# Branch sum before weight piece: a new order of the splits in the last two branch steps of a two-layer decoder

## The reference

```python
h = rms_norm(x, norm1_g[l])
P = h @ w_in[l]                        # all queries, keys, values and gates
o_a, o_b, o_c = window_attention, block_attention, gated_linear_attention   # each 256 x 512
g = sigmoid(gates)                     # 3 gates of 256 x 1024
y = g[0] * (o_a @ w_branch_a) + g[1] * (o_b @ w_branch_b) + g[2] * (o_c @ w_branch_c)
x = x + y @ w_o
x = x + FFN(rms_norm(x, norm2_g[l]))   # layer 0: SwiGLU of 2816; layer 1: top 2 of 8 experts of 1408
```

## Time and profile before

| what | value |
|---|---|
| median of 3 runs | 1080.41 us (1075.01 to 1085.00) |
| profiled execution: time | 1086.16 us |
| profiled execution: span of the trace | 1084.40 us |
| busy TensorE, VectorE, ScalarE (share of the span) | 98%, 48%, 37% |
| mean granted TensorE clock | 0.978 of full speed |

### The profile page before, as it was taken

How to read it: one execution, slowest core, us unless ns; L and a number is a source line. 1 busy time by engine, 2 the same in 40 slices (tenths; PEclk the granted TensorE clock), 3 DMA queues, 4 the chain that set the end, 5 groups by cost and what they waited for, 6 DMA issues and landing times.

```text
span 1084.4 us, 21913 instructions
## 1 busy us (share of the span) xinstructions
PE 1057.7 (98%) x9653; PEld 873.4 (81%) x9653; DVE 519.7 (48%) x751; ACT 402.6 (37%) x619; POOL 17.0 (2%) x61
## 2 busy tenths in 40 slices
PE   8999999998999999999999999799999999999996
PEld 7998999998999999999899999796554563563552
DVE  5565776576467565456578655735112111111112
ACT  5554655535354453457346553331111011011012
POOL 3000000000000000000000000010000000000000
PEclk8999999999999999999999999888999999999999
DMA  6553643664556475555345449696999999999991
GB/s 212 173 163 91 185 147 117 182 207 141 170 176 179 152 221 197 164 159 172 111 141 162 145 133 343 209 350 218 390 401 398 404 402 398 402 404 398 399 363 40
DMA packets 131278, 255.38 MB, mean 236 GB/s; under 512 B 7505, under 2 KB 80241, under 8 KB 131186
## 3 DMA queue, kind: packets, MB, share of 16 engines
q1 hardware_dynamic: 130322, 252.41, 66.8%
q10 hardware_dynamic: 864, 1.59, 0.4%
HBM read 252.93 MB, written 1.05 MB: 234 GB/s over the span
## 4 chain that ended last, share of the span: by engine, by line
PE 89%; DMA 4%; DVE 2%; SPq 2%; ACT 2%; issue 1%; ACTq 0%; DVEq 0%
PE ps L1579 33%; PE ps L1574 16%; PE ps L1576 15%; PE ps L1575 15%; PE ps L1568 3%; PE ps L1570 3%; PE ps L1569 3%; SPq L553 2%; DMA e_ring<-in_moe_w_down 2%; ACT w_hi L690 1%; DMA raw<-in_w_o 1%; DVE w_lo L984 1%; PE ps L1787 1%; DMA x<-in_x 1%; DVE xhat L1241 0%
## 5 line engine op out<-in xcount | busy, mean ns | idle before, releaser
L984 DVE TENSOR_TENSOR w_lo<-raw,w_hi 128x1536 fp32r<-128x1536 f32 (+2 forms) x157 | 248.6, 1604 | 141.0 <-ACT w_hi L690 140.8
L690 ACT ACTIVATE w_hi<-raw 128x1536 fp32r<-128x1536 f32 (+2 forms) x157 | 210.5, 1361 | 158.3 <-DMA raw<-in_w_in 81.4
L1574 PE MATMUL ps<-hT_hi,w_hi 128*128 128x256 f32 (+1 forms) x752 | 217.4, 289 | 8.0 <-DVE hT_lo L1033 3.6
L1575 PE MATMUL ps<-hT_lo,w_hi 128*128 128x256 f32 (+1 forms) x752 | 213.6, 284 | 0.0
L1576 PE MATMUL ps<-hT_hi,w_lo 128*128 128x256 f32 (+1 forms) x752 | 213.6, 284 | 0.0
L1579 PE MATMUL ps<-e_ring,xe 128*32 128x352 f32 (+2 forms) x2560 | 199.6, 462 | 0.0
L1579 PEld LDWEIGHTS ps<-e_ring,xe 128*32 128x32 f32 x2560 | 106.0, 110 | 83.3 <-issue 56.0
L1574 PEld LDWEIGHTS ps<-hT_hi,w_hi 128*128 128x128 f32 (+1 forms) x752 | 143.1, 190 | 12.5 <-issue 6.9
L1576 PEld LDWEIGHTS ps<-hT_hi,w_lo 128*128 128x128 f32 (+1 forms) x752 | 143.2, 190 | 0.5
L1575 PEld LDWEIGHTS ps<-hT_lo,w_hi 128*128 128x128 f32 (+1 forms) x752 | 143.2, 190 | 0.4
L1579 PE MATMUL ps<-e_ring,ehT 128*32 128x512 f32 x880 | 101.3, 593 | 1.1 <-DMA e_ring<-in_moe_w_down 1.1
(11 more groups left out here) (330 smaller groups left out, 1426.7 us busy)
## 6 DMA issues: line engine op xcount, KB each, us to landing
e_ring<-in_moe_w_gate SPq DMA_DIRECT2D x64, 704.0 KB, 12.5
e_ring<-in_moe_w_up SPq DMA_DIRECT2D x64, 704.0 KB, 12.8
e_ring<-in_moe_w_down SPq DMA_DIRECT2D x88, 512.0 KB, 12.3
raw<-in_w_in SPq DMA_DIRECT2D x56, 768.0 KB, 4.3
raw<-in_w_in SPq DMA_DIRECT2D x20, 512.0 KB, 3.6
raw<-in_ffn_w_gate SPq DMA_DIRECT2D x12, 768.0 KB, 4.5
raw<-in_ffn_w_up SPq DMA_DIRECT2D x12, 768.0 KB, 4.4
raw<-in_ffn_w_down SPq DMA_DIRECT2D x12, 768.0 KB, 4.4
```

The costliest lines, as they stand in the source:

```text
L690: act.activation(slot(n, "hi", k), slot(n, "raw", k), ACT.Copy).then_inc(hi_done, 1)
L984: dve.tensor_tensor(slot(n, "lo", k), slot(n, "raw", k), slot(n, "hi", k).bitcast(F32), ALU.subtract).then_inc(lo_done, 1)
L1574: pe.matmul(out, wh, hi, start=first, stop=False, skip_group_check=True)
L1575: pe.matmul(out, wh, lo, start=False, stop=False, skip_group_check=True)
```

## The change

Branch steps 7 and 8 are entered in `BEHIND` with 0 splits at their head, so that their one split comes after their own work. On ScalarE the copy of a group of `y` moves from the end of its own step into the next one (group 0 into step 7, group 1 into step 8, group 2 to the head of step 0 of the output projection).

```diff
-BEHIND = {("wof", 2): 1, ("down", DOWN_END[0]): 0, ("down", DOWN_END[1]): 0}
+BEHIND = {("branch", 7): 0, ("branch", 8): 0, ("wof", 2): 1, ("down", DOWN_END[0]): 0, ("down", DOWN_END[1]): 0}
...
+            def y_high(l, s):
+
+                k0, k1 = OCOLS[s][0] // P, sum(OCOLS[s]) // P
+                act.wait_ge(y_ready, y_banks(l, s))
+                act.activation(hT_hi[:, k0:k1, :], xT[:, k0:k1, :], ACT.Copy).then_inc(y_hi_done, 1)
+
...
                     n, p, a, _ = FIRST[l, step]
+                    if name in ("wo", "wof") and i == 0:
+                        y_high(l, 2)
                     for u in splits_before(l, step):
                         split_hi(u)
...
-                    elif name == "branch" and i >= 6:
-                        k0, k1 = OCOLS[i - 6][0] // P, sum(OCOLS[i - 6]) // P
-                        act.wait_ge(y_ready, y_banks(l, i - 6))
-                        act.activation(hT_hi[:, k0:k1, :], xT[:, k0:k1, :], ACT.Copy).then_inc(y_hi_done, 1)
+                    elif name == "branch" and i >= 7:
+                        y_high(l, i - 7)
```

## The result

The changed kernel takes 1066.89 us (median of 4 runs, 1064.39 to 1068.31) against 1078.60 us for the kernel before (median of 4, 1075.01 to 1085.0): ratio 0.9875, 95% interval 0.9844 to 0.9905, so 13.5 us less (10.2 to 16.8). The two medians by themselves lie 11.7 us apart; the ratio on record is used from here on. Both kernels ran again on another chip: ratio 0.9864 (0.9848 to 0.988), 14.7 us less (13.0 to 16.4). So the changed kernel is faster, by a little over 1%. The forecast was 1066.2 us, 14.2 us less. The profiled execution after is 1068.31 us, its span 1066.6 us.

A forecast was written before the change was run, and what follows sets the result against it. TensorE, busy 98% of the span, was taken as the bound, with waits from two weight splits in the chain. Layer 0's 6.2 plus layer 1's 8.0 us made 14.2 off 1080.41: 1066.2 us, range 1060 to 1076.

The forecast's parts named there:

- part 1: ScalarE's instruction sequence and waits stay the same, cost 0; only VectorE's order is new.
- part 4: Work queued behind the moved splits: later sums 1.4 us late at cost 0; loads cost 0, up to 1 us in layer 1.
- part 2: VectorE in layer 0: both TensorE holes (1.04 and 3.68 us) close and the lower clock goes, gaining 6.2 us.
- part 3: VectorE in layer 1: holes and slow clock total 9.1 us, 1.1 us of waiting remains, gaining 8.0 us.
- The clock: TensorE's lower clock behind the second hole goes in both layers: 1.5 us in layer 0, 2.6 in layer 1.
- The rival that it would not: The clock does not come back, so 1.5 + 2.6 us are not gained: 1070.3 us; chance 0.13.
- part 5: Expert loads and their stream move earlier with TensorE, so the whole gain is kept to the end; 2 us either way for clock.
- The swallowing expert stage: Expert-load stream has an unmoving anchor and swallows layer 1's part, only layer 0 counting: 1074.2 us; chance 0.12.
- The change does not do what it says: At step 1, TensorE waits for a weight piece instead of `y`; unit 51 has 1.5 us slack: 1080 us; chance 0.06.
- Slower: Remaining waits leave the whole output projection, 22.6 us a layer, at half clock: 1102 us; chance 0.03.

The follow-up runs named there:

- the two kernels with ScalarE's old code: Kernel before with VectorE's new order in one layer each, ScalarE unchanged: ratio 0.9928 for layer 0, 0.9946 for layer 1.
- layer 0 alone: Kernel before with VectorE's new order in layer 0 only, ScalarE's code old: ratio 0.9928 to the kernel before, 7.8 us less.
- before again: The unchanged kernel before, run once more for a second profile: 1081.67 us, span 1079.9 us.
- the router's filling: Changed kernel plus four unread identity matmuls among the router's matmuls of 8 columns: ratio 0.9866 to the kernel before.
- the filled holes of layer 0: Kernel before with 3 and 13 unread identity matmuls in TensorE's two holes of layer 0: ratio 0.9977, 2.5 us less.
- step 8 alone: Kernel before with VectorE's new order in branch step 8 only, both layers: ratio 0.992, 8.6 us less.
- step 7 alone: Kernel before with VectorE's new order in branch step 7 only, both layers: ratio 0.9916, 9.1 us less.
- layer 1 alone: Kernel before with VectorE's new order in layer 1 only, ScalarE's code old: ratio 0.9946 to the kernel before, 5.8 us less.
- the kernel with all holes filled: Kernel before with unread identity matmuls in TensorE's holes, 4 and 15 in layer 0, 13 and 12 in layer 1: ratio 0.9989, 1.2 us less.

## Why the prediction was right

**Only VectorE's order is new (part 1).** Right: the two kernels with ScalarE's old code add up to the whole gain, within their intervals. So was part 4, which put the later sums of step 0 at no cost: they start at 249.23, 1.1 us behind TensorE's end of that step, and no wait follows.

**Layer 0 (part 2).** Forecast 6.2 us, measured 6.45 by the same matmuls in the two traces, and 7.8 (4.7 to 10.8) in the timed runs with layer 0 alone. The trace adds what the forecast did not count in this layer: a low stretch behind the second norm, granted clock 0.60 before and 1.00 after, worth 1.5. Together 6.45 + 1.5 = 7.95. In the second profile of before all of it stands in one place: from the last branch matmul to step 1 it takes 16.39 us, against 15.09 in the first and 8.64 after, so 7.75. The working holds in its steps: Y0's low part was forecast to be done at 237.5 and was at 237.46; G7 at 239.65 and at 239.58; unit 50 at 241.4 and at 241.25; Y1 at 242.3 and at 242.12; Y2 at 245.0 and at 244.84. Durations from single rows of before, laid end to end, were good to 0.2 us over 8 us.

**Layer 1 (part 3).** Forecast 8.0 us. In the profiled pair it is (707.43 - 689.75) - (689.76 - 681.29) = 9.2, where 707.43 is the first matmul of step 1 before; the timed runs give 5.8 (3.7 to 8.1). The 1.1 us of remaining waits did not come, since unit 152 landed sooner after: step 6's products stood 681.29 - 675.62 = 5.67 us ahead of the branches' end, where it was 689.75 - 685.24 = 4.51 before. The profile with the router's filling shows that this term was well worked out: with the late landing the waits were 0.28 and 0.61 us, forecast 0.25 and 0.85.

What was off is the time of before. The forecast took one execution's hole, and its low stretch behind it, for the kernel's. From the last branch matmul to step 1 the first profile of before takes 17.80 us. Three other profiles with VectorE's old order in layer 1 take 15.94 (the filled holes of layer 0), 15.74 (before again) and 14.01 (layer 0 alone); the two of the changed kernel take 8.59 and 8.55. So layer 1 is worth 9.2 us by the pair and 5.4 to 7.4 by the others. That difference of 2 to 4 us is about what lies between 17.8 us in the profiled pair and 13.5 to 14.7 in the timed runs.

**The sum** came out nearer than its parts. By the timed runs layer 0 brought 7.8 where 6.2 were forecast, and layer 1 5.8 where 8.0 were: the errors had opposite signs, and that 14.2 fits the 13.5 and 14.7 so well is in part luck. Both intervals are wide enough to hold the forecast parts.

**The clock.** Forecast 4.1 us of the 14.2. In layer 0 1.5 + 1.5 by the traces, 2.5 (1.1 to 3.9) measured by itself with filled holes. In layer 1 the clock came back too (1.00 in all of step 0), but what that brought is not measured by itself. The rival that it would not has fallen: even where the short waits came, in the profile with the router's filling, the granted clock stayed at 1.00. The Trainium skill, page "TensorE: Matmul & The Clock Gate", section "A second HAM failure mode: psum-queue depth-cycling", has the clock swing when TensorE idles for a very short time between groups of matmuls often enough. No run here has frequent idles of that kind. Of single idles the traces give no length that decides. Behind waits of 1.85 us (step 8 alone), 2.0 (layer 0 alone) and 2.2 (step 7 alone) in layer 1 the granted clock fell to 0.50 within about a microsecond. Behind waits of 2.3 us (before again), 2.5 (the filled holes of layer 0) and 3.15 (before) in layer 1 it stayed at 1.00 up to the second hole, and behind 1.71 in layer 0 (step 7 alone) through all of step 0.

**Kept to the end (part 5).** Right, by the ladder of SyncE's queue and by the kernel with layer 1 alone. The swallowing expert stage has fallen.

**The change does not do what it says.** The slack of unit 51 is 1.5 us as forecast; the rival fell because nothing used it up. Beyond the slack the one wait measured cost twice itself, as that rival said. **Slower** has fallen with the clock. Its 22.6 us a layer are 192 x 0.118; at the 0.123 of its next sum they would be 23.6, and nothing else hangs on them.

**The reason in its wording was too narrow.** "Two weight splits stand inside a chain that needs neither" is true, and taking them out gives all of the gain. But leaving them in and bringing ScalarE to VectorE's order gives 10.8 us (7.7 to 14.0). The prediction saw VectorE wait for ScalarE's copy, and never priced that wait of 2.29 us apart from the split of 1.76.

**What stays open.** Why the low stretch around the router and its length differ from run to run; why the kernel with all holes filled gains only 1.2 us with its clock at 1.00; and what decides whether the clock falls after a single idle.

## What to carry to other kernels

Where two engines work one after the other on the same pieces, and TensorE waits for one of them, write down both engines' orders beside each other: an opposite order costs the second engine the first one's whole time for the other piece, and either engine's order can mend it. Lay the moved instructions end to end with durations from single rows and set them against TensorE's due times; that was good to 0.2 us here. Before a hole of one profiled execution goes into a sum at its full size, ask what it starts from, and take a second profile: a hole behind a load is as long as that load happened to be late, and the low clock behind it varies too.

## What the runs showed of the hardware

**The run time follows the clock.** In 17 runs of the kernel before on one chip the time falls with the mean granted clock (correlation -0.89) by 0.70 us for each 0.001: 1073.95 and 1075.67 us at 0.990, 1078.7 to 1081.5 at 0.983 to 0.984, 1080.8 to 1082.4 at 0.980 to 0.981. The changed kernel's profiled executions do the same, a span of 1066.6 us at 0.984 and of 1060.9 at 0.992. So the differences between runs of one kernel go for the most part with TensorE's clock.

**Where it differs** is the router and what follows. The groups of TensorE between 700 and 745 in the profile of the changed kernel hold the 32 gather matmuls so (total us, mean ns):

```profile
L1585 PE MATMUL ps<-sel,rows 128*128 128x160 f32 x32 | 7.1, 417 | 0.0
```

and in the second profile of the very same kernel so:

```profile
L1585 PE MATMUL ps<-sel,rows 128*128 128x160 f32 x32 | 3.8, 278 | 0.1
```

The busy time from 690 to 750, of the first and then of the second (the granted clock stands third from the end):

```profile
690.00:750.00 60.00, 60.00 (x513) 44.66 (x515) 25.50 (x104) 15.13 (x38) 3.48 (x11) 0.86 0.82 305
```

```profile
690.00:750.00 60.00, 58.50 (x583) 41.18 (x585) 25.96 (x106) 15.43 (x39) 3.48 (x11) 0.97 0.89 332
```

TensorE is busy for the full 60 us in the execution in which the clock is 0.86 on the mean. It falls there at 708, behind 18 us in which the engine shows no idle time, so an idle engine is not what shows ahead of it. In the other execution the fall, at 716, comes with an idle stretch of 1.4 us and lasts some 3 us only. In the one profile with four identity matmuls among the router's, the gathers took 7.1 us too.

**A transfer's time is not constant.** The same 768 KB load, unit 152, took from 4.9 to 6.9 us from issue to ScalarE's first use in fourteen profiles. In the five in which VectorE has the old order in step 7 and nothing fills layer 1's holes, the hole behind it grew with that time:

| profile | issue to use, us | hole, us |
|---|---|---|
| step 8 alone | 5.0 | 1.85 |
| layer 0 alone | 5.1 | 2.0 |
| before again | 5.5 | 2.3 |
| filled holes of layer 0 | 5.7 | 2.5 |
| before | 6.8 | 3.15 |
